# Placing ScalarE's half of a top-k threshold search between projection tiles: an even spread over 60 half slots against a table by TensorE's time

## What is computed

```
sc = indexer_scores(qib, wib, ki, valid[None])
_, sel = lax.top_k(sc, topk)
return sparse_attend(qb, take_rows(k, sel), take_rows(v, sel), sel <= qpos[None, :, None])
```

## Time and profile before

| | |
|---|---|
| median of three runs | 2822.25 us (2822.1 to 2825.87) |
| the profiled execution: its own time | 2825.47 us |
| its span in the trace | 2823.7 us |
| PE busy | 2717.1 us, 96% |
| DVE / POOL / ACT busy | 42% / 33% / 30% |
| share of PE in the chain that ended last | 86% |
| mean granted clock of PE | 0.984 |

### The profile page before, as it was taken

How to read it: one execution, slowest core, us unless ns; L and a number is a source line. 1 busy time by engine, 2 the same in 40 slices (tenths; PEclk the granted TensorE clock), 3 DMA queues, 4 the chain that set the end, 5 groups by cost and what they waited for, 6 DMA issues and landing times.

```text
span 2823.7 us, 46763 instructions
## 1 busy us (share of the span) xinstructions
PE 2717.1 (96%) x17946; PEld 2490.3 (88%) x17946; DVE 1178.5 (42%) x2925; ACT 845.7 (30%) x1616; POOL 919.9 (33%) x709
## 2 busy tenths in 40 slices
PE   5878999999999999999999999999999999999999
PEld 4736874667889999999999899999899999999999
DVE  7488958664253222222222343333622222222233
ACT  4155646774153111111111531111621111111113
POOL 3402653342044222222222542232532222222221
PEclk8999999999999999999999999999999999999999
DMA  8203567103330111111111021202111111111101
GB/s 302 77 15 120 180 211 251 40 1 111 96 92 11 49 50 49 47 48 49 48 49 49 8 60 45 60 16 60 45 46 45 45 45 45 45 45 45 45 15 63
DMA packets 206062, 192.23 MB, mean 68 GB/s; under 512 B 32480, under 2 KB 183880, under 8 KB 205418
## 3 DMA queue, kind: packets, MB, share of 16 engines
q1 hardware_dynamic: 205930, 190.42, 22.2%
HBM read 175.43 MB, written 14.96 MB: 67 GB/s over the span
## 4 chain that ended last, share of the span: by engine, by line
PE 86%; DVE 5%; SPq 2%; issue 2%; ACT 2%; DMA 1%; POOL 1%; DVEq 0%; ACTq 0%
PE PS L354 72%; PE PS L1805 2%; PE PS L1834 2%; PE PS L1816 2%; DVE s_all L1502 1%; PE PS L393 1%; PE PS L873 1%; DVE na L484 1%; SPq L799 1%; PE PS L2639 1%; PE PS L886 1%; SPq L798 1%; PE PS L1821 1%; ACT na L508 1%; POOL hlo L520 0%
## 5 line engine op out<-in xcount | busy, mean ns | idle before, releaser
L354 PE MATMUL PS<-hhi,uhi 128*128 128x352 f32 (+1 forms) x3240 | 1064.4, 329 | 26.8 <-DVE hlo L1257 10.8
L354 PE MATMUL PS<-hhi,ulo 128*128 128x352 f32 (+1 forms) x3240 | 1046.1, 323 | 0.0
L354 PE MATMUL PS<-hlo,uhi 128*128 128x352 f32 (+1 forms) x3240 | 1045.4, 323 | 0.0
L354 PEld LDWEIGHTS PS<-hhi,uhi 128*128 128x128 f32 (+1 forms) x3240 | 611.8, 189 | 47.9 <-issue 30.5
L354 PEld LDWEIGHTS PS<-hlo,uhi 128*128 128x128 f32 (+1 forms) x3240 | 613.5, 189 | 3.4 <-issue 0.2
L354 PEld LDWEIGHTS PS<-hhi,ulo 128*128 128x128 f32 (+1 forms) x3240 | 611.8, 189 | 0.8
L2321 POOL TENSOR_TENSOR alo<-af,ahi 128x352 fp32r<-128x352 f32 x132 | 125.6, 952 | 1022.3 <-ACT ahi L2268 1022.3
L2377 DVE TENSOR_TENSOR af<-sg,PS 128x352 f32<-128x352 f32 x132 | 68.8, 521 | 876.8 <-PE PS L354 869.8
L354 PE MATMUL PS<-ahi,dhi 128*128 128x352 f32 x1248 | 419.4, 336 | 4.7 <-DVE y L577 3.8
L354 PE MATMUL PS<-ahi,dlo 128*128 128x352 f32 x1248 | 403.3, 323 | 0.0
L354 PE MATMUL PS<-alo,dhi 128*128 128x352 f32 x1248 | 402.2, 322 | 0.0
(11 more groups left out here) (297 smaller groups left out, 2815.5 us busy)
## 6 DMA issues: line engine op xcount, KB each, us to landing
wraw<-in_ffn_w_gu_dram SPq DMA_DIRECT2D x88, 512.0 KB, 7.5
wraw<-in_ada_w_dram SPq DMA_DIRECT2D x80, 512.0 KB, 4.8
draw<-in_ffn_w_down_dram SPq DMA_DIRECT2D x44, 512.0 KB, 4.3
wraw<-in_conv_w_in_dram SPq DMA_DIRECT2D x24, 512.0 KB, 7.0
adaw<-in_ada_w_dram SPq DMA_DIRECT2D x16, 512.0 KB, 12.6
wraw<-in_attn_w_out_dram SPq DMA_DIRECT2D x48, 128.0 KB, 3.1
y_scratch<-y SPq DMA_DIRECT2D x1, 4224.0 KB, 12.3
xst<-in_x_prompt_dram SPq DMA_DIRECT2D x4, 1024.0 KB, 7.1
```

Of the source, the lines that this page charges most:

```text
L354: last = pe.matmul(out, w(kt), x(kt), start=(n == 0), stop=(n == 3 * count - 1))
```

## The change

The half slot of each count comes from a table, `COUNT_AT`. The table numbers PE's work through the 39 items, 10 units for a key or query item and 7 for a V item, with half slots in the middle and at the end of each item. Count h goes into the first half slot at 24 + 4.9 h units or more.

```diff
+V_ITEMS = range(ITEM_AT[6], ITEM_AT[6] + 9)
+
+
+def count_halves():
+
+    ends = list(itertools.accumulate(7 if i in V_ITEMS else 10 for i in range(N_ITEMS)))
+    at = [0.5 * x for i, b in enumerate(ends) for x in (2 * b - (7 if i in V_ITEMS else 10), 2 * b)]
+    return [next(s for s, t in enumerate(at) if t >= 24 + 4.9 * h) for h in range(64)]
+
+
+COUNT_AT = count_halves()
...
             for h in range(64):
-                if 4 + 60 * h // 64 == half:
+                if COUNT_AT[h] == half:
```

More of the change, by code:

```diff
@@ L8 @@
+import itertools
 from contextlib import ExitStack
```

## The result

| | before | changed |
|---|---|---|
| median of the runs beside each other, us | 2822.18 (6 runs, 2820.26 to 2828.62) | 2812.14 (6 runs, 2807.08 to 2814.85) |
| profiled execution, its span, us | 2825.47, 2823.7 | 2813.62, 2811.8 |

The ratio of changed to before is 0.9958, with a 95% interval from 0.9945 to 0.9971: faster by 8 to 16 us. 2807.9 was forecast, with a range of 2804.5 to 2814.5. Over all 27 runs of it the median is 2808.8 us, over all 72 of the kernel before 2820.8. The difference of the means is **12.7 us** (95% interval 10.9 to 14.5), where the forecast had 14.4. Of the 72 runs, 22 (median 2823.71 us) had no run of the changed kernel beside them; on the three occasions with both kernels the differences of the means are 11.9, 11.8 and 12.7 us, together 12.1 (10.4 to 13.8).

A forecast was written before the change was run, and what follows sets the result against it. PE, 86% of the chain, bounds the kernel; time is won only where it waits or runs slowly. 15.4 us at chunk 15 less 1.0 at the search's end is 14.4: 2822.25 to 2807.9 us, range 2804.5 to 2814.5.

The forecast's parts named there:

- Part 1: Items 11 to 14: evacuations come on time, so PE's waits of 0.65, 1.04, 1.24 and 6.06 us go.
- rival 3: Items 11 to 15: ACT still waits for candidates ahead of evacuations, nothing is gained, 2823 us; chance 0.05.
- Part 2: Item 15: PE takes chunk 15 15.4 us earlier, after a 1.5 us wait; chunk 14's wait of 2.61 us goes.
- the train: Ahead of chunk 15's load: weight 10's split, its low part on POOL, chunk 14, nine stores, weight 12; 1.5 us wait.
- The bound of 17.2 us: Item 15: upper bound on the 15.4 us lead, if chunk 15 came in time.
- Rival 1: Behind chunk 15's wait, an item at half clock, price 1.5 us: gain 12.9, time 2809.4 us; chance 0.12.
- Part 3: Items 15 to 34: no gain or loss; ACT's loop of 4.6 us fits in an item of 5.2 us.
- rival 2: Late iterations each cost 0.3 us more than their item, 6 us over 20 items: 2814.3 us; chance 0.08.
- rival 4: Items 11 to 34: loop of ACT and DVE outlasts an item; at 0.9 us excess 2829 us, slower; chance 0.03.
- Part 4: End of the search: it ends 1.2 us after PE's first scores want it, a loss taken as 1.0 us.
- the tail: Search work on DVE after its loop ends, before attention's first step: taken as 10.94 us.

The follow-up runs named there:

- e6: Changed kernel with counts 0 to 23 placed as in the kernel before, the other 40 as changed: 2823.89 us, 1.0005 of the kernel before.
- e4: Changed kernel with the nine stores of V one step later, behind chunk 17 instead of chunk 14: 2806.3 us, 0.9955 of the kernel before.
- e10: Changed kernel with counts every 4.7 units instead of 4.9, second run of this edit: 2805.26 us, 0.9945 of the kernel before.
- e1: The changed kernel run again, no edit: 2808.8 us, 0.9958 of the kernel before.
- e9: The changed kernel run a third time, no edit: 2807.93 us, 0.9954 of the kernel before.
- e8: Changed kernel with 17 unused products added in PE's gaps at attention's start: 2806.08 us, 0.9943 of the kernel before.
- e2: Changed kernel with counts every 4.7 units instead of 4.9, first run of this edit: 2806.5 us, 0.9956 of the kernel before.
- e3: Changed kernel with counts every 5.1 units instead of 4.9: 2813.57 us, 0.9978 of the kernel before.
- e5: The kernel before, profiled again, no edit: 2818.34 us.
- e12: The kernel before, profiled a third time, no edit: 2818.28 us.

## Why the prediction was right, and which term was not

**Part 1, right.** The waits of 0.65, 1.04, 1.24, 6.06 and 2.61 us went, and e6 brings them back with the first 24 counts alone, and takes the whole gain with it. So the gain comes from counts that stood ahead of evacuations in items 4 to 14, as forecast, and rival 3 (nothing moves) is out.

**Part 2, right in its size.** A lead of 15.4 us and a wait of 1.59 us, against 15.4 and 1.5. e4 shows that the train was read rightly: with the stores behind the chunks, the wait is gone. The bound of 17.2 us for a chunk in time, 1.8 us beyond 15.4, holds too: counted from chunk 14, e4 takes chunk 15 1.7 us earlier. In the medians it does not show.

Rival 1, half clock behind chunk 15, held in some profiles and not in others. After the wait of 1.59 us the clock was 1.00, and likewise in e10 after 1.38, in e1 after 1.55, in e9 after 1.86 and in e8 after 2.00 us. In e2, after 1.98 us, three microseconds ran at 0.51, and in e3, after 2.06 us, at 0.54. In e2 the next chunk came 6.74 us later and not 5.17, so the price of 1.5 us was right.

**Part 3, right.** DVE follows PE's items with waits of a third of a microsecond, and no excess is handed on. The last L1598 came within 0.1 us of the forecast, measured from the stage's start, so rivals 2 and 4 did not occur.

**Part 4, the term that was mis-sized.** Its first half, the late start, was put at 1.2 us after PE's first scores want it, and I took 1.0. It measures 0.58 us (1.29 us of idle time against 0.71); the missing 0.6 us is the tail, which I took at 10.94 us and which took 10.31. Its second half, "up to 1.5 us, if the longer gap keeps PE at half clock for one more item's worth of work", was the wrong size, and I took none of it. From second scores to the sixteenth reciprocal the changed kernel takes 49.8 us in the mean of three profiles, the kernel before 44.9: 4.9 us, of which 2 in the best profile and 6.3 in the other two. The lead of 15.0 us at the second scores (213.11 against 198.09 us into the stage, means of three) is 10.2 us at the sixteenth pair.

That these 4.9 us are slower work and not waits is shown by PE's busy and idle time in the stretch: for the same 370 or so matmuls it is busy for 40.2 us before and 45.0 us with the change (means of three profiles each), and idle for 4.7 and 4.8 us. The granted clock goes with it, as in e1's window from 404 to 414, where PE is busy for all of its 10 us at 0.50. That filling the idle time shortens the half clock is what e8 shows, in one profile: with the same end of the search, 3.4 us at half and a stretch of 46.47 us. e8 fills gaps in pairs 0 and 1 as well, so it does not show how much the one gap of 1.29 us does. For that stand e2 and e10, where the search ends in time and the gap is 0.7 us: 10.2 us at half, a lead of 13.6 us at the sixteenth pair (258.02 less 244.43), and some 2 us less in the whole time. As the table's groups touch, they make it likely that the wider gap lengthens the half clock, and do not prove it. I had counted the 21 us that DVE had to spare as cover that can be used up to its end. The last microsecond of it seems to be worth two or three.

The Trainium skill says of this (TensorE: Matmul & The Clock Gate, "Loop structure matters more than you think") that long waits for loads between matmuls make PE run cold. At chunk 15, the wait for a load where I weighed it, the traces have it both ways, cold in e2 and e3 and not in five others. At attention's start PE did run cold, but most waits there are for DVE, POOL and ACT, of 0.5 to 1.3 us, which the rule does not speak of.

**What stays open.** First, with the same gap of 1.29 us one profile has 10.2 us at half clock and another 27.3; no run tells what decides, and whether the gap decides at all rests on eleven profiles. Second, the three profiled executions of each kernel differ by 10.1 us in the mean (2820.70 against 2810.59), all runs by 12.7; the profiles of one kernel lie up to 7 us apart, so six do not settle the rest. The 0.58 us and 4.9 us taken from 15.4 leave 9.9, what the profiles show; the runs' 12.1 to 12.7 lie between that and the forecast of 14.4. That 2807.9 agrees so well with the medians of e1 and e9 is in part luck: the kernel before stood at 2820.4 and 2821.3 us beside them, not at the 2822.25 that the forecast starts from.

## What to carry to other kernels

Work on an in-order engine that waits for a third engine belongs where the evacuations behind it are not yet wanted; placing it by the waiting engine's time was worth 0.45% here. Place it so that its last step still comes before the next stage wants it: 4.7 units instead of 4.9 moved the end of the search from 0.6 us too late to 5.5 us too early and won some 2 us more, at the edge of what the runs can tell. Where a stretch starts with small products and short waits on PE, as attention does here, idle time can be paid for twice, once as such and once in the clock, so cost a gap there by the clock's rows behind it and not by its length, and take more than one profile.

## What the runs showed of the hardware

The granted clock can differ behind the same wait. Some 300 us after the search, at the start of the sample's attention, PE waits 1.9 to 2.5 us for a load of the cached keys, in either kernel. Behind it the kernel before ran 13.6 us at half clock (10.2 in e5 and e12). In e6 the clock stayed at 1.00, and so it did in e9 and e3, after waits of 2.02 and 1.95 us. PE's row of the wait and the window behind it, of the kernel before and of e6:

```profile
697.62 0.66 PE L1676 MATMUL PS<-ident,Kr 128*128 128x128 f32 x4 [2.48 <-DMA Kr<-in_cache_k_dram]
```

```profile
700.00:710.00 10.00, 10.00 (x79) 8.74 (x76) 1.54 (x4) 2.77 (x7) 2.36 (x1) 0.50 0.35 104
```

```profile
701.29 0.66 PE L1690 MATMUL PS<-ident,Kr 128*128 128x128 f32 x4 [1.93 <-DMA Kr<-in_cache_k_dram]
```

```profile
700.00:710.00 10.00, 8.71 (x95) 6.92 (x96) 2.37 (x7) 2.64 (x7) 3.11 (x2) 1.00 0.53 145
```

Here e3 and e6 got back a part of what they had lost, in their profiles. e6 is 5.1 us behind the kernel before at the sixteenth pair (263.13 against a mean of 258.02); at DVE's fourth reciprocal of the sample's attention, some 40 us behind this wait, it is level (541.42 us into the stage, against a mean of 541.52). e3 is 8.5 us behind the changed kernel at the wait (497.84 against 489.36) and 5.1 us at that reciprocal (534.76 against 529.65). Both reached this place late, but so did e1 and e4, 2.7 to 3.5 us behind the first profile of the changed kernel, and they ran 10.2 us at half clock behind the same wait. Why the clock holds in one case stays open. For a reader of profiles it means that 3 to 5 us lost in one stretch of this kernel can come back in another, and no run found a cause for it in the code.
